# Which output slots of the two wide mixers run token tile by token tile: the last three or the last two

## What is computed

```
x = _layer_norm(ALPHA * x + mix, ln_g[i, 0], ln_b[i, 0])
ffn = _moe(x, router_w, router_b, w_gate[i], w_up[i], w_down[i])
x = _layer_norm(ALPHA * x + ffn, ln_g[i, 1], ln_b[i, 1])
x = x + sigmoid(x @ ple_w_gate[i] + ple_b_gate[i]) * (p[i] @ ple_w_proj[i])
```

## Time and profile before

| | us |
|---|---|
| median of 3 runs | 1584.76 |
| the three runs | 1584.45, 1584.76, 1587.28 |
| the profiled execution: time | 1586.1 |
| the profiled execution: span, first to last instruction | 1583.9 |
| PE busy in that span | 1554.8 (98%) |
| DVE busy | 741.2 (47%) |
| mean traffic | 337 GB/s |

### The profile page before, as it was taken

One profiled execution on the slowest core, in us unless ns is written; L12 is line 12 of the kernel. 1 busy time (PEld: TensorE's weight loads), 2 busy tenths in 40 slices (PEclk: granted clock), 3 DMA queues, 4 the chain that ended last, 5 costly groups with the idle time before them and its releaser, 6 DMA issues.

```text
span 1583.9 us, 17795 instructions
## 1 busy us (share of the span) xinstructions
PE 1554.8 (98%) x7376; PEld 912.4 (58%) x7384; DVE 741.2 (47%) x1203; ACT 503.3 (32%) x644; POOL 45.5 (3%) x47
## 2 busy tenths in 40 slices
PE   9999999999999999999999999999999999999998
PEld 7874333378877743333788887633334887433335
DVE  4672232294757622221956755612225666232217
ACT  5522222154433213221544443122212552132113
POOL 0000000000000000001020000000000000000010
PEclk9999999999999999999999999999999999999999
DMA  9899999966536999999755557799999678999992
GB/s 362 344 381 387 420 422 421 420 267 256 185 133 239 377 365 422 421 422 420 288 229 203 186 212 316 321 398 421 421 420 411 236 276 353 365 422 420 422 420 93
DMA packets 75146, 534.40 MB, mean 337 GB/s; under 512 B 8976, under 2 KB 9264, under 8 KB 10544
## 3 DMA queue, kind: packets, MB, share of 16 engines
q1 hardware_dynamic: 73728, 530.94, 82.8%
q0 software_dynamic: 1328, 2.21, 0.4%
HBM read 532.06 MB, written 1.05 MB: 337 GB/s over the span
## 4 chain that ended last, share of the span: by engine, by line
PE 88%; DMA 6%; DVE 3%; ACT 1%; issue 1%; SPq 0%; ACTq 0%
PE psum L1134 37%; PE psum L736 12%; PE psum L738 12%; PE psum L737 12%; DMA expert_work<-in_experts 6%; PE psum L747 3%; PE psum L1144 2%; PE psum L887 2%; PE psum L1121 1%; PE psum L1081 1%; DVE w_lo L1654 1%; PE psum L1074 1%; PE psum L1126 1%; PE psum L1183 1%; PE psum L1026 1%; PE psum L971 1%
## 5 line engine op out<-in xcount | busy, mean ns | idle before, releaser
L1654 DVE TENSOR_TENSOR w_lo<-raw,w_hi 128x2048 fp32r<-128x2048 f32 (+1 forms) x124 | 257.4, 2093 | 179.6 <-ACT w_hi L1353 179.1
L736 PE MATMUL psum<-w_hi,xT_hi 128*128 128x512 f32 x672 | 264.9, 394 | 0.5 <-DVE w_lo L1654 0.5
L738 PE MATMUL psum<-w_hi,xT_lo 128*128 128x512 f32 x672 | 261.8, 390 | 0.0
L1353 ACT ACTIVATE w_hi<-raw 128x2048 fp32r<-128x2048 f32 (+1 forms) x124 | 214.2, 1747 | 149.9 <-PE psum L738 113.1
L737 PE MATMUL psum<-w_lo,xT_hi 128*128 128x512 f32 x672 | 261.5, 389 | 0.0
L1353 ACT ACTIVATE work<-psum 128x512 f32<-128x512 f32 x152 | 85.8, 596 | 312.3 <-PE psum L747 212.7
L1134 PE MATMUL psum<-raw,xg 128*64 128x512 f32 x656 | 153.2, 594 | 1.1 <-DMA raw<-in_experts 1.1
L1654 DVE TENSOR_TENSOR work_r<-psum,work_r 128x512 fp32r<-128x512 f32 (+1 forms) x100 | 67.6, 689 | 180.1 <-ACT spare_r L1353 96.0
L1134 PE MATMUL psum<-expert_work,xg 128*64 128x512 f32 x608 | 141.4, 595 | 4.4 <-ACT work L1353 2.7
L736 PEld LDWEIGHTS psum<-w_hi,xT_hi 128*128 128x128 f32 x672 | 126.2, 188 | 27.0 <-DVE w_lo L1654 0.9
L738 PEld LDWEIGHTS psum<-w_hi,xT_lo 128*128 128x128 f32 x672 | 126.1, 188 | 26.4
(11 more groups left out here) (188 smaller groups left out, 1549.9 us busy)
## 6 DMA issues: line engine op xcount, KB each, us to landing
expert_work<-in_experts SPq DMA_DIRECT2D x126, 1024.0 KB, 15.2
raw<-in_experts SPq DMA_DIRECT2D x122, 1024.0 KB, 16.5
raw<-in_slots SPq DMA_DIRECT2D x116, 1024.0 KB, 4.9
expert_high<-in_experts SPq DMA_DIRECT2D x64, 1024.0 KB, 12.0
expert_spare<-in_experts SPq DMA_DIRECT2D x24, 1024.0 KB, 10.4
expert_norm<-in_experts SPq DMA_DIRECT2D x20, 1024.0 KB, 10.4
expert_bias<-in_experts SPq DMA_DIRECT2D x20, 1024.0 KB, 10.9
lent<-in_slots SPq DMA_DIRECT2D x4, 1024.0 KB, 5.8
```

The lines of the kernel that those rows point to most:

```text
L736: mm(out, lhs[0], rhs[0], start=start, stop=False)
L738: return mm(out, lhs[1], rhs[0], start=False, stop=stop)
L1353: return nc.scalar.activation(dst, src, func)
L1654: return tt(lo, whole, hi.bitcast(F), ALU.subtract)
```

## The change

One slot of the last group, the third last, is taken out of the loop over tiles and done for both tiles before it. Nothing else is edited; the sums take the same products in the same order.

```diff
             def last_rows(L, n, count, lhs):
 
+                rows_both(n, count, lhs, count - 3)
                 for t in range(T):
-                    for i in range(1, 4):
+                    for i in range(2, 4):
                         rows_slot(n, count, lhs, count // 4 - 1, t, i, mix_done)
                 transpose_tile(3 * L + 1, 0)
```

## The result

The change makes the kernel slower. Its median is 1591.72 us (six runs, 1590.7 to 1593.86) against 1584.67 for the kernel before (six runs beside it, 1584.45 to 1587.28): ratio 1.0045, 95% interval 1.0035 to 1.0055, or about +7.0 us. The direction is as predicted; the size lies above the forecast of 1588.8 and just above the range, which ended at 1591.4.

The account below looks back on a forecast made before the run. PE is busy 98% of the span, but DVE's layer norm sets the pace at the mixers' ends. 1584.76 + 2.71 for the later layer norm + 1.36 for one more clock fall = 1588.8 us; range 1585.8 to 1591.4.

Parts of the forecast that it names:

- DVE's chain in layer 1: End of layer 1's mixer: tile 0's later layer norm delays tile 1's addition and all up to the gather, +1.87 us.
- DVE's chain in layer 2: End of layer 2's mixer: PE's 1.06 us wait for the lent slot goes, but tile 1's layer norm comes 0.84 us later.
- The standstill: Before tile 1's transposes in layers 1 and 2: PE stands still about 1.45 us, waiting for DVE's layer norm.
- The early loads at nothing: Two loads per layer go out two steps (5.44 us) earlier as the third last slot is freed sooner; cost nothing.
- How many falls: Light stretches of layers 1 and 2: one more fall of PE's clock in the two together, chance 0.40.
- The price of a fall: Tile 1's logits to the gather: a fall of PE's clock costs 1.36 us, bounds nothing and 1.6.
- The case of no further fall: Rival: the clock holds in layers 1 and 2, only the later layer norm counts, 1587.5 us; chance 0.30.
- a hidden delay: Rival: PE is the bound and DVE's delay is hidden, 1583.7 us, or 1584.8 if experts' waits swallow it; chance 0.08.
- The lower end of the range: Whole kernel: 1585.8 us, said to lie below the case of no fall by the spread of the runs.

Follow-up runs that it names:

- nine fillers: The change with nine filler matmuls in place of two before tile 1's transposes in layers 1 and 2: 1587.7 us, ratio 1.0016.
- late release: The change, but the third last slot's buffers are given free one product into tile 1's next step, about where they were before: 1593.91 us, ratio 1.0047.
- spatial mixer alone: The kernel before with the edit in layer 2 only: 1589.61 us, ratio 1.0028.
- kernel without fillers: The kernel before without the two filler matmuls ahead of tile 1's transposes in layers 1 and 2: 1588.22 us, ratio 1.0030.
- norm row held back: The kernel before with GpSimd's broadcast of layer 2's norm row held back until DVE has split the lent slot: 1583.48 us, ratio 0.9989.
- one filler: The change with one filler matmul between tile 1's transposes and its logits: 1591.53 us, ratio 1.0044.
- retention alone: The kernel before with the edit in layer 1 only: 1590.97 us, ratio 1.0035.

## Why the prediction was right and where it was wrong

**DVE's chain in layer 1: right.** Tile 0's transposes wait for DVE until 544.09, which is 0.72 after the end of the steps (543.14 + 0.23), as worked out. The +1.87 came out as 16.07 - 14.30 = 1.77, read with nine fillers, where the clock is out of it. It is 0.07 under the lower bound: tile 1's addition overlaps tile 0's last instruction by 0.08 (544.01 against 544.09), not by 0.05, and DVE's work for tile 1 was 0.05 shorter (544.01 to 551.41 against 541.50 to 548.95).

**DVE's chain in layer 2: right.** PE gets to the end without the wait for the lent slot, and the 1.06 us end in a wait for DVE, as predicted. The net is 1.76 - 1.06 = 0.70 where I took 0.84.

**The standstill: right.** 1.28 and 1.29 us of idle time, where I said about 1.45, in both layers.

**The early loads at nothing: right**, by the kernel with the late release.

**How many falls: about right.** I took one more fall in the two layers together. In layer 1 the clock fell in all four profiles that have the edit there and no extra fillers over the standstill; in layer 2 in two of four. Of the four profiles of each layer with the steps of before and at least their fillers, it fell in none. The mean granted clock of the six runs of the change was 0.994 in the two of 1593.8 and 1593.9 us, and 0.996 or 0.997 in the other four; the profile of the late release, with both falls, has 0.993, and the four profiles with the edit and one fall have 0.996 or 0.997. In the spatial mixer alone five of six runs have 0.995 to 0.997. By that two runs of six had both falls. This is argued from means, not seen in a trace.

**The price of a fall: wrong.** The step that failed is "A fall so costs 1.36 us; bounds are nothing ... and 1.6". I measured it on the one fall that the trace of before held, in which the clock fell when tile 1's logits were done and came back after some 3 us. I took the length of that one as the length of any, and the upper bound from it too. The runs show 1.36 again in layer 1 of the kernel without fillers and in layer 0 of the one with the norm row held back, but 3.0 in layer 1 of the change and 4.24 in layer 2 alone. In the ten falls that the profiles hold in these routes, each priced against the same stretch without one (14.30, 16.06 or 16.07 us), the price goes with the time for which the clock stayed at 0.50: a little over 3 us in those of 1.36, about 7 us in those of 2.67 to 3.04, about 10 us in those of 4.02 to 4.26, so some 0.4 us for each us at 1.2 GHz. The short ones began when tile 1's logits were done, those of 7 us in tile 1's transposes or logits, those of 10 us in the standstill or as it ended, which is where the change put new idle time. Why a fall that begins earlier lasts longer, no run here shows. The forecast was 4.07 us over the kernel before and the measured medians differ by 7.05; of the 3.0 between them the price makes up 1.6, DVE's chain takes off 0.2, and the rest is told of below.

With the measured terms the sum is 1584.67 + 2.47 + 3.0 = 1590.1 for a run with a fall in layer 1, and 1594.4 with 4.24 more for a run with both. The runs came at 1590.7 to 1592.0 and at 1593.8 and 1593.9.

**What stays open.** The four runs that by their clocks had a single fall lie 0.6 to 1.8 us above 1590.1, the other two 0.5 to 0.6 below 1594.4. The profiled execution, at 1592.0, is one of the four, and its fall of 3.0 us is in the sum: what it lacks lies outside the two routes. The largest piece is the stretch from the gather of layer 2 to the last matmul of layer 3's mixer, 1342.53 - 1020.51 = 322.02 us against 1335.79 - 1015.23 = 320.56 before. In the five profiles whose layer 2 has the steps of before it takes 320.51 to 321.87 us, so it varies by over a microsecond without the edit. In the other executions what is over could also be a longer fall (20.09 us to the gather in layer 1 with one filler, 1 us more than in the profiled execution); no run tells these apart there. On the average nothing is missing: 2.47 + 3.0, and 4.24 more in two runs of six, make 6.9 us, and the means of the six runs each differ by 1592.2 - 1585.1 = 7.0. Nor is it settled why layer 2 keeps its clock in some executions. The Trainium skill, page "TensorE: Matmul & The Clock Gate", section "Part 1: The HAM clock gate (the "warmup" mystery)", says of the warm-up at a kernel's start that the monitor runs freely, so that the moment of the change differs from run to run of the same kernel. The traces agree in so far as the same work met a fall in layer 2 in two of four profiles, and in layer 1 met it in the logits in two (the change, retention alone), in the transposes in one (late release) and in the standstill in another (one filler).

**The rivals.** The case of no further fall, 1587.5, is what the fillers make of the change: 1587.7. That of a hidden delay is out: DMA stands at 0.00 where the delay would have had to be paid back. The lower end of the range, 1585.8, does not follow from its words: 2.8 us, the spread of the three runs, below 1587.5 is 1584.7.

## What to carry to other kernels

An engine that hands two tiles one after the other to another engine sets the distance between them: here three steps of 2.72 us per tile just covered DVE's 7.4 us, two do not, and a wait removed on the busiest engine then only moves to the next one. Where such a wait falls among short matmuls, price the clock with it: cover it with fillers, or reckon with a longer fall than the one that happens to be in the trace. And where an instruction takes longer than its neighbours of the same shape, look at what ran beside it before moving work out of its way.

## What was not expected of the hardware

- Two filler matmuls of 0.21 us in each of two layers are worth 3.3 us of the kernel's time: without them the granted clock fell to 0.50 in both layers, though PE idled for only 0.36 us there.
- A fall has no fixed price: 1.36, 3.0, 3.04 and 4.24 us were measured in the same piece of program, about 0.4 us for each us that the clock stayed at 0.50.
- A broadcast on GpSimd of 2.29 us made a DVE split of 2.29 us take 4.08, although the two write different buffers.
